# VectorE's low halves two key blocks ahead instead of three, and activation stores three blocks later in SyncE's queue, in a hybrid attention, SSD and expert-retrieval layer

## What is computed

```python
act = gelu(einsum('nd,nhkd->nhk', t, u_tab[e]))
out = einsum('nhk,nhkd->nd', g * act, v_tab[e])
```

## Time and profile before

| | |
|---|---|
| median of three runs | 2450.03 us |
| profiled execution's own time | 2446.26 us |
| its span | 2444.5 us |
| busy: TensorE, VectorE, ScalarE, GpSimd | 88%, 64%, 31%, 33% |
| up part before the slabs, key blocks 0 to 79 | about 1040 to 1376 us |
| slab stage | about 1377 to 1688 us |
| tail | 1688 to 1745 us |
| value stage | about 1750 to 2400 us |

### The profile page before, as it was taken

One profiled execution on the slowest core, in us unless ns is written; L12 is line 12 of the kernel. 1 busy time (PEld: TensorE's weight loads), 2 busy tenths in 40 slices (PEclk: granted clock), 3 DMA queues, 4 the chain that ended last, 5 costly groups with the idle time before them and its releaser, 6 DMA issues.

```text
span 2444.5 us, 34439 instructions
## 1 busy us (share of the span) xinstructions
PE 2149.1 (88%) x12253; PEld 1783.6 (73%) x12253; DVE 1570.6 (64%) x3259; ACT 748.1 (31%) x1111; POOL 808.3 (33%) x499
## 2 busy tenths in 40 slices
PE   7979999998769979999999888888889898998983
PEld 7978995554433439999999888888767676676662
DVE  1256215554452331199888677875888888989888
ACT  2122113443330012243444445443232323223221
POOL 2323320001110013366666511111634445565550
PEclk9989998999879989999999998998899899998996
DMA  9999987885995552155555666667999999999992
GB/s 349 347 350 350 346 305 316 320 316 199 320 338 187 181 199 87 51 166 169 174 169 169 209 244 228 236 230 261 359 394 394 393 393 376 393 394 394 394 371 100
DMA packets 200412, 682.81 MB, mean 279 GB/s; under 512 B 18432, under 2 KB 84352, under 8 KB 194304
## 3 DMA queue, kind: packets, MB, share of 16 engines
q1 hardware_dynamic: 151696, 508.36, 59.2%
q0 software_dynamic: 46080, 167.79, 18.1%
q10 hardware_dynamic: 2544, 5.48, 0.6%
HBM read 618.78 MB, written 196.32 MB: 333 GB/s over the span
## 4 chain that ended last, share of the span: by engine, by line
PE 34%; DMA 23%; issue 21%; DVE 14%; ACT 4%; POOL 3%; SPq 0%; ACTq 0%; DVEq 0%; POOLq 0%
DMA overlay<-peer_v 15%; PE bank L188 7%; PE bank L189 7%; PE bank L190 7%; DMA overlay<-peer_u 5%; DVE arena L1775 3%; DVE overlay L1952 3%; PE bank L1762 2%; POOL overlay L341 2%; PE bank L586 2%; PE bank L602 2%; DVE arena L1770 2%; POOL overlay L1401 2%; PE bank L625 1%; PE bank L652 1%
## 5 line engine op out<-in xcount | busy, mean ns | idle before, releaser
L188 PE MATMUL bank<-overlay 128*128 128x384 f32 (+4 forms) x2856 | 993.6, 348 | 145.2 <-DVE overlay L1956 88.4
L189 PE MATMUL bank<-overlay 128*128 128x384 f32 (+4 forms) x2856 | 973.0, 341 | 0.0
L190 PE MATMUL bank<-overlay 128*128 128x384 f32 (+4 forms) x2856 | 970.7, 340 | 0.0
L188 PEld LDWEIGHTS bank<-overlay 128*128 128x128 f32 x2856 | 561.2, 196 | 207.3 <-issue 112.3
L190 PEld LDWEIGHTS bank<-overlay 128*128 128x128 f32 x2856 | 558.7, 196 | 33.8
L189 PEld LDWEIGHTS bank<-overlay 128*128 128x128 f32 x2856 | 561.0, 196 | 30.5
L1401 POOL TENSOR_TENSOR overlay<-overlay 128x1024 fp32r<-128x1024 f32 x99 | 265.7, 2685 | 208.2 <-ACT overlay L1393 208.2
L1610 POOL DMA_INDIRECT arena<-peer_rows,arena x160 | 182.3, 1139 | 430.2 <-DVE arena L1770 410.3
L1610 POOL DMA_INDIRECT arena<-peer_v,arena x160 | 229.5, 1434 | 171.6 <-DVE arena L1775 158.8
L1775 DVE SCALAR_TENSOR_TENSOR arena<-arena 128x1024 f32<-128x1024 f32 x160 | 204.5, 1278 | 0.4
L1770 DVE SCALAR_TENSOR_TENSOR arena<-arena 128x1024 f32<-128x1024 f32 x160 | 193.7, 1218 | 7.2 <-DMA arena<-peer_rows,arena 7.2
(11 more groups left out here) (221 smaller groups left out, 2095.1 us busy)
## 6 DMA issues: line engine op xcount, KB each, us to landing
overlay<-peer_u SPq DMA_DIRECT2D x128, 512.0 KB, 3.7
overlay<-peer_v SPq DMA_DIRECT2D x128, 512.0 KB, 13.0
o_ks<-cache_k SPq DMA_DIRECT2D x16, 4088.0 KB, 27.4
o_vsall<-cache_vall SPq DMA_DIRECT2D x16, 4088.0 KB, 39.6
arena<-cache_kT SPq DMA_DIRECT2D x32, 896.0 KB, 11.2
arena<-cache_v SPq DMA_DIRECT2D x56, 512.0 KB, 6.8
arena<-w_out SPq DMA_DIRECT2D x48, 512.0 KB, 4.8
act<-arena SPq DMA_DIRECT2D x128, 192.0 KB, 1.9
```

Source lines behind the costliest of these rows:

```text
L188: pe.matmul(out, lhs[0], rhs[0], start=start, stop=False)
L189: pe.matmul(out, lhs[0], rhs[1], start=False, stop=False)
L190: return pe.matmul(out, lhs[1], rhs[0], start=False, stop=stop)
```

## The change

`LEAD` goes from 3 to 2, and a new `KEEP_LAG = 3` puts the store of block a - 3 where that of block a stood.

```diff
-        LEAD = 3
+        LEAD, KEEP_LAG = 2, 3
...
             def next_row(a):
                 if a + 4 < PK:
                     fetch(a + 4, a % 4, (u_lo, QF + a + 1) if a < EARLY + LEAD else (u_lo2, a - (EARLY + LEAD) + 1))
-                keep(a, a % 4, a // 4)
+                if a >= EARLY + KEEP_LAG:
+                    keep(a - KEEP_LAG, (a - KEEP_LAG) % 4, (a - KEEP_LAG) // 4)
...
+            for a in range(PK - KEEP_LAG, PK):
+                keep(a, a % 4, a // 4)
```

## The result

The changed kernel took 2377.7 us (median of five runs, 2373.41 to 2379.3), the kernel before beside it 2447.36 us; the ratio is 0.972, 95% interval 0.9703 to 0.9736. The forecast was 2395 us, in a range of 2383 to 2426: right in its direction, 17 us too slow, and the time lies 5 us outside the range.

A forecast was written before the change was run, and what follows sets the result against it. The prediction took the slab stage to be held by waits behind a late load, the value stage by bytes. Terms 10 x 4.7 + 4.7 + 1 + 2 = 54.7, say 55 us, off 2450.0 gave 2395 us; range 2383 to 2426.

The forecast's parts named there:

- What bounds the slab stage: Slabs: a loop of store, late load, cast, low part, hot steps and copies, 25.3 us a period.
- The new period, 20.6 us: Slabs: TensorE's 19.8 us plus a 0.6 us hole, taken as 20.6 for handing over; 4.7 us less a period.
- the hole of 0.6 us in every slab: TensorE at hot step 5: ready at 11.1 us, but copy 1 ends at 11.7.
- The clock: Slabs: clock stays full, since it was still 1.00 behind 2.41 us of idleness and the expected hole is 0.6.
- A slow stretch of 3: TensorE in the old slabs: 6 us at clock 0.50 behind the 3.31 us hole lose another 3 us.
- the clock still falls: Rival, slabs: small holes stay and TensorE loses up to 3 us a slab; 2411 us, chance 0.24.
- Transfers of one queue in turn: SyncE's queue in the slabs: transfers are served in order, so the burst leaves the first load's 9.7 us unchanged.
- The slower rival: Slabs: transfers sharing the queue side by side land the first load 4 us later; 2473 us, chance 0.07.
- They are no earlier now: Tail: its loads still come behind four loads of peer_v, activations and a slab; ScalarE's 16.2 us wait at block 120.
- 4.7 + 2 us: Gains expected in the eleventh period (4.7) and the tail (2); at most 5.5 and 5.9.
- bytes hold most of it: Tail: DMA share is 0.95, so of at most 5.9 us to be had only 2 were taken.
- The value stage passes the gain on: Value stage: starts when block 127 is stored and moves the same bytes, so the gain passes in full.

The follow-up runs named there:

- opening the loop at the load: Kernel before (LEAD 3, stores in their old place) with a slab's first load put ahead of the slab store: 2389.4 us, ratio 0.9766.
- The filler's kernel: Kernel before with ten more fp32 matmuls of constants on TensorE before hot step 4 in each slab: 2443.4 us, ratio 0.9983.
- the second pair: Second profiles of the kernel before and the changed kernel, both unchanged: 2446.2 us and 2380.0 us.
- Putting the loads back: Changed kernel with SyncE's first four loads of peer_v made to wait for Gelu of block 115: 2385.2 us, ratio 0.9759.
- a stage made 7 us faster still: Changed kernel with a slab's first load ahead of the slab store in the queue: 2376.3 us, ratio 0.9724.

## Why the prediction was wrong

- **What bounds the slab stage: right.** Load, cast, low part, hot step, in this order; the wait chain went, and opening the loop at the load gave the same.
- **The new period, 20.6 us: right**, 20.5 measured (20.6 in the second profile), and 47 us for ten periods against 47.9. What should be late next came too: short waits for copies (6.8 us in all), ScalarE's wait for peer_u unchanged. Only the hole of 0.6 us in every slab is a hole of about 1 us in every other one.
- **The clock: right in its outcome, on thinner ground than it seemed.** From the first slab store to the last it stayed at 1.00 with holes of up to 1.4 us. The filler's kernel had 0.50 behind a hole of 1.74 us, so 2.41 us was not a safe length. TensorE: Matmul & The Clock Gate (A second HAM failure mode) of the Trainium skill has short idle times make the clock swing; the changed kernel's six holes do not show it, the four slow periods with the filler do. "A slow stretch of 3" is right for TensorE, but it cost the old period about 1.3. What it would have cost in the changed kernel no run shows, so the price of the rival "the clock still falls" stays untested.
- **Transfers of one queue in turn: right.** With six transfers issued in a burst the first load's cast came 9.65 us behind the slab store on average, against 9.58 before. The slower rival is out. DMA: Bandwidth & Descriptors (Queues, rings and completion order) of the Trainium skill has descriptors of one ring consumed in order; the two averages agree.
- **"They are no earlier now": the step that failed.** I went through SyncE's queue in the slabs, where moving the stores gains nothing (true with LEAD 3: 25.4 us with the stores alone; with LEAD 2 it gains 3.5 us in ten periods), and then took the tail's first loads as fixed. The store of block 115 was the one thing that held four loads of peer_v back until its Gelu. With it moved they left 8.5 us earlier in relation to the last slab store. The eleventh period and the tail were put down for 4.7 + 2 us; they brought 6.9 + 6.4, and the gap 1.1 (not there in the second pair). The low end of the range allowed 5.5 + 5.9 for them. In the eleventh period the 2.1 us that SyncE spent issuing those loads ahead of the last slab store were overlooked, though the earlier trace rows had the 28.3. In the tail "bytes hold most of it" was wrong too: the changed tail takes 49.9 us, no more than TensorE's 50.4 us of work. Putting the loads back cost 12.6 us. That LEAD 2 alone makes the tail 8.7 us longer was not foreseen either; the stores' place covers it.
- **The value stage passes the gain on: right**, as far as two profiles of each kernel tell.
- **The size.** The terms came to 54.7 us, of which 1, for slab 0, was ahead of the first store and is not there; the trace shows 62. This alone would have given 2450.0 - 62 = 2388 us, inside the range; that the time lies outside it is also due to what follows. The medians differ by 69.7, and by 66.2 for the repeated kernels (2446.2 and 2380.0). The 4 to 8 us more lie ahead of the slabs or in the value stage and change from execution to execution; they are not put down to any part of the change. The first median of before, 2450.0, was also 3 to 10 us above the later ones (2439.6 to 2447.4).

## What to carry to other kernels

When an issue is moved in a queue, go through everything behind its old place, to the end of the stage and beyond, and ask of each what now holds it; a wait that costs nothing in the steady part can be the one that holds back the next stage's transfers. Two edits that work on neighbouring bounds are not additive: here 40.6 and 8.6 us alone, 62.4 together, and a stage made 7 us faster still gained nothing, since the tail behind it gave 8 us back. A slow clock costs only as much as TensorE is part of the path, here about 1.3 us of its 3 (an estimate from the periods with the filler); filling the hole is a cheap way to find out, if the periods are then compared one by one and not by their average.

## What was not expected of the hardware

The issue of a 512 KB load by SyncE takes 0.43 us most often where it stands alone or right behind the slab store, but mostly 0.9 to 1.5 us, once 2.15, further back in a burst. As the next issue behind the gates' load it took 1.44 us in the kernel before, 3.69 in the changed kernel, and 6.76 in the kernel with the first load ahead of the store and the tail's loads moved. No other row of SyncE falls into these 6.76 us. Why they differ is not tested.
